# One lot of values per pair of heads, the maximum taken before a copy, and two output products interleaved

## The reference, cut to what matters

```python
def even_mixer(h_lat, h_ctx, ...):
    ...                                   # keys and values: context and latent tokens joined, 768 in all
    def merge(o_a, o_b):
        return jnp.dot(jnp.concatenate([o_a, o_b], axis=-1), w_out)
    out_lat = merge(attend(mla_q(...), ka, va), attend(gqa_q(...), kb, vb))
    out_ctx = merge(attend(mla_q(... ctx), ka_c, va_c), attend(gqa_q(... ctx), kb_c, vb_c))

def attend(q, k, v):                      # per block of 128 queries and per head
    s = einsum(q, k) * scale
    p = softmax(s)
    return einsum(p, v)

x = x + gt1 * out_lat
ctx = ctx + cgt1 * out_ctx
```

## Time and profile before

| | us |
|---|---|
| runs of the kernel before | 3757.66, 3762.18, 3762.24; median 3762.18 |
| profiled execution, device time | 3759.26 |
| its span, first to last instruction | 3757.9 |
| PE busy over the span | 3628.1 (97%) |
| DVE, ACT, POOL busy | 2474.8 (66%), 1597.5 (43%), 259.1 (7%) |
| mean granted TensorE clock | 0.974 of full speed |

### The profile page before, as it was taken

How to read it: one execution, slowest core, us unless ns; L and a number is a source line. 1 busy time by engine, 2 the same in 40 slices (tenths; PEclk the granted TensorE clock), 3 DMA queues, 4 the chain that set the end, 5 groups by cost and what they waited for, 6 DMA issues and landing times.

```text
span 3757.9 us, 53327 instructions
## 1 busy us (share of the span) xinstructions
PE 3628.1 (97%) x21516; PEld 3086.6 (82%) x21516; DVE 2474.8 (66%) x3727; ACT 1597.5 (43%) x2587; POOL 259.1 (7%) x197
## 2 busy tenths in 40 slices
PE   7999999999999998999999999999999999979999
PEld 4866778888888866788889987899978999659998
DVE  5445667755547255544598877888756887478886
ACT  3246643323135234323354446544444444475443
POOL 0000104830000010000000011000020000100000
PEclk8999999999999989999999999999999999999999
DMA  5210022433322101223233332333323334203332
GB/s 211 99 32 1 2 88 83 133 125 127 121 86 74 58 29 42 83 95 101 90 96 102 102 107 79 96 102 101 96 91 124 111 103 146 63 16 93 106 106 91
DMA packets 276309, 338.94 MB, mean 90 GB/s; under 512 B 15456, under 2 KB 197344, under 8 KB 275424
## 3 DMA queue, kind: packets, MB, share of 16 engines
q1 hardware_dynamic: 272752, 320.40, 27.4%
q10 hardware_dynamic: 3312, 15.13, 1.1%
HBM read 329.18 MB, written 6.29 MB: 89 GB/s over the span
## 4 chain that ended last, share of the span: by engine, by line
PE 82%; DVE 7%; ACT 2%; issue 2%; DMA 0%; SPq 0%; POOL 0%; ACTq 0%; DVEq 0%
PE ps L843 15%; PE ps L845 15%; PE ps L844 15%; PE ps L1667 7%; PE ps L1669 7%; PE ps L1668 7%; PE ps L2128 1%; PE ps L2102 1%; PE ps L1987 1%; PE ps L1988 1%; PE ps L1989 1%; DVE t L442 1%; PE ps L2092 1%; PE ps L3259 1%; PE ps L3257 1%
## 5 line engine op out<-in xcount | busy, mean ns | idle before, releaser
L843 PE MATMUL ps<-t 128*128 128x512 f32 (+1 forms) x2236 | 806.2, 361 | 10.4 <-DVE t L2853 6.5
L844 PE MATMUL ps<-t 128*128 128x512 f32 (+1 forms) x2236 | 801.5, 358 | 0.0
L845 PE MATMUL ps<-t 128*128 128x512 f32 (+1 forms) x2236 | 800.4, 358 | 0.0
L429 ACT ACTIVATE t<-t 128x1024 fp32r<-128x1024 f32 (+2 forms) x438 | 437.1, 999 | 588.6 <-PE ps L845 367.3
L442 DVE TENSOR_TENSOR t<-t 128x1024 fp32r<-128x1024 f32 (+2 forms) x438 | 506.2, 1157 | 244.7 <-ACT t L429 242.0
L1667 PE MATMUL ps<-blocks_hi,t 128*128 128x256 f32 x1888 | 533.0, 282 | 16.2 <-ACT t L1696 12.1
L1668 PE MATMUL ps<-blocks_lo,t 128*128 128x256 f32 x1888 | 528.8, 280 | 0.0
L1669 PE MATMUL ps<-blocks_hi,t 128*128 128x256 f32 x1888 | 528.7, 280 | 0.0
L843 PEld LDWEIGHTS ps<-t 128*128 128x128 f32 x2236 | 426.6, 191 | 75.6 <-issue 10.7
L845 PEld LDWEIGHTS ps<-t 128*128 128x128 f32 x2236 | 426.3, 191 | 62.2
L844 PEld LDWEIGHTS ps<-t 128*128 128x128 f32 x2236 | 426.8, 191 | 61.2 <-issue 1.1
(11 more groups left out here) (499 smaller groups left out, 6274.6 us busy)
## 6 DMA issues: line engine op xcount, KB each, us to landing
t<-w_s_up SPq DMA_DIRECT2D x184, 256.0 KB, 3.6
t<-w_up SPq DMA_DIRECT2D x88, 512.0 KB, 3.6
raw_more<-w_s_up SPq DMA_DIRECT2D x168, 256.0 KB, 3.5
t<-w_ada SPq DMA_DIRECT2D x160, 256.0 KB, 3.1
raw_more<-w_s_down SPq DMA_DIRECT2D x72, 256.0 KB, 2.7
t<-w_down SPq DMA_DIRECT2D x32, 512.0 KB, 3.6
t<-w_s_down SPq DMA_DIRECT2D x56, 256.0 KB, 2.7
t<-w_ada SPq DMA_DIRECT2D x16, 512.0 KB, 10.6
```

The costliest lines, as they stand in the source:

```text
L429: k.A.activation(self.pair(n)[0], self.slot(self.raw_at[n])[:, 0:self.size(n)], ACT.Copy)\
L843: k.T.matmul(out, wh, hh, start=(i == 0), stop=False)
L844: k.T.matmul(out, wh, hl, start=False, stop=False)
L845: ins = k.T.matmul(out, wl, hh, start=False, stop=(i == len(kts) - 1))
```

## The change

In `PairUnits`: `pe_spread` is merged into `pe_values`, and a pair's values are done in one lot in the even step, after the spread; the odd step has scores and transposes alone. DVE takes the maximum of unit i before it copies unit i-2, and forms the result of a pair in the even step, behind that copy. In `ProjectOut`, which gets a flag `paired` that only the first attention sets, the first two blocks are done side by side: `dense_two` goes over kt and does three matmuls for block 0 and three for block 1, first for the latent tokens, then for the context tokens; both weight blocks are let go of when all four products are done. The next blocks are as before.

```diff
 class ProjectOut:
+    def made(self, m, si):
+        if self.paired and m < 2:
+            return self.done.at(2 * si + m + 1)
+        return self.done.at(self.ns * m + si + 1)
+
+    def pe_pair(self):
+        k, st = self.k, self.k.stream
+        weights = [st.operand(self.c + m, self.name, m) for m in range(2)]
+        for si, mix in enumerate(self.mixes):
+            outs = []
+            for m in range(2):
+                i = self.ns * m + si
+                self.bank[i], before = k.banks.take(self.res.at(i + 1))
+                k.pe.wait_ge(before)
+                outs.append(self.bank[i][:, 0:(NL, NC)[si]])
+            dense_two(k, outs, weights, mix.k, lambda kt: self.ready(si, kt), (self.done, self.done))
+        for m in range(2):
+            st.used[self.c + m] = self.done.at(2 * self.ns)
+
     def pe(self, between=None):
         k, st = self.k, self.k.stream
+        if self.paired:
+            self.pe_pair()
         for m in range(8):
-            w = st.operand(self.c + m, self.name, m)
+            w = st.operand(self.c + m, self.name, m) if m > 1 or not self.paired else None
             if between:
                 between(m)
+            if w is None:
+                continue
...
-                k.dve.wait_ge(self.done.at(i + 1))
+                k.dve.wait_ge(self.made(m, si))
...
-            if 0 <= i - 4 < n:
-                if i % 2 == 0:
-                    self.pe_spread((i - 4) // 2)
-                self.pe_values((i - 4) // 2, i % 2)
+            if i % 2 == 0 and 0 <= i - 4 < n:
+                self.pe_values((i - 4) // 2)
...
-    def pe_values(self, p, part):
+    def pe_values(self, p):
...
-        for c in range(part * nb // 2, (part + 1) * nb // 2):
+        for c in range(nb):
...
-        if part:
-            ins.then_inc(self.pv.sem, 1)
+        ins.then_inc(self.pv.sem, 1)
...
         for i in range(n + 4):
+            if i < n:
+                self.dve_max(i)
             if 0 <= i - 2 < n:
                 self.dve_keep(i - 2)
-            if i < n:
-                self.dve_max(i)
-            if i % 2 and 0 <= i - 4 < n:
+            if i % 2 == 0 and 0 <= i - 4 < n:
                 self.dve_result((i - 4) // 2)
```

More of the change, by code:

```diff
@@ L1902, with __init__ @@
 class ProjectOut:
-    def __init__(self, k, name, mixes, ready, scale, scale_ready, following=None):
+    def __init__(self, k, name, mixes, ready, scale, scale_ready, following=None, paired=False):
         self.k, self.name, self.mixes, self.ready, self.scale, self.scale_ready = k, name, mixes, ready, scale, scale_ready
+        self.paired = paired
         self.done, self.res = k.event("out_done"), k.event("out_residual")
@@ L2104, in pe_turn @@
         ins.then_inc(self.tn.sem, 1)
-    def pe_spread(self, p):
-        k = self.k
-        k.pe.wait_ge(self.fin.at(p))
-        k.pe.wait_ge(self.rc.at(2 * p + 2))
-        for half in range(2):
-            ins = k.T.matmul(k.ps[64 * half:64 * half + 64, 6 + (p + 1) % 2, 128:256],
-                             self.recip(p)[:, half:half + 1].broadcast_to([P, 64]), k.ident, start=True, stop=True)
-        ins.then_inc(self.rb.sem, 1)
-    def pe_values(self, p, part):
+    def pe_values(self, p):
         k = self.k
@@ L2120, in pe_values @@
         b = k.ps[:, 6 + p % 2, :]
+        k.pe.wait_ge(self.fin.at(p))
+        k.pe.wait_ge(self.rc.at(2 * p + 2))
+        for half in range(2):
+            ins = k.T.matmul(k.ps[64 * half:64 * half + 64, 6 + (p + 1) % 2, 128:256], self.recip(p)[:, half:half + 1].broadcast_to([P, 64]),
+                             k.ident, start=True, stop=True)
+        ins.then_inc(self.rb.sem, 1)
         k.pe.wait_ge(self.rk.at(p))
@@ L2829, in even_mixer @@
             out = ProjectOut(k, "att_out", [M, MC], lambda si, kt: hl.at(8 * si + kt + 1), lambda m, si: k.mod(0, 2, m, si),
-                             ada.ready(0, 2), lambda finished: Gather(k, finished, 2))
+                             ada.ready(0, 2), lambda finished: Gather(k, finished, 2), True)
             def pe_program():
```

## The result

The changed kernel takes 3766.25 us (median of 14 runs, 3754.87 to 3770.93) beside 3758.26 us (14 runs, 3753.24 to 3762.24) for the kernel before. The profiled spans are 3764.7 and 3757.9 us, 6.8 apart as well.

A forecast was written before the change was run, and what follows sets the result against it. PE was taken to set the pace, DVE and ACT mattering only as latencies. Latent rounds -2.2, grouped rounds +4.8 and projection +2.1 summed to +4.7 us, forecast 3765.4 us, range 3750 to 3774.

The forecast's parts named there:

- The copy binds on grouped heads: Grouped even steps: transposes wait 0.46 us for DVE's copy behind the maximum; a pair takes 5.16 for 4.97.
- The ends of the wide run: First narrow and first wide units of a round: grouped transposes wait 0.92, 0.47 and 1.3 us for copies.
- the loop of 2.74: Grouped heads, DVE's path from scores through maximum and copy until PE can start the transposes: 2.74 us.
- Sum of the attention: Attention stage: grouped rounds lose 4.8 us, latent rounds gain 2.2, together +2.6 us.
- A change of output width costs 0.12 and 0.16: PE groups beside a 64/128-column change cost 0.12 and 0.16 us more; one lot saves 0.28 a pair.
- the margin of 0.11: Latent heads, start of scores to next transposes: PE's path 3.43 us, DVE's 3.32, so no wait, whole saving kept.
- Projection: PE waits 2.1 us at L807: Column sums ahead of block 3 wait for DVE's last multiply-add after the late weight release; cost +2.1 us.
- the upper bound of 3.7: Projection: the most its wait could cost, 3.7 us, if SyncE's second tile takes 5.1 us.
- Rival 1: Attention: the copy doesn't bind, every pair gets its 0.28 us; 3748.0 to 3750.9 us; chance 0.20.
- Rival 2: Attention: DVE's result waits in every wide pair for ACT's spread copy; +9.6, 3773.6 to 3776.5 us; chance 0.18.
- Rival 3: Projection: its wait isn't there; 3761.9 to 3764.8 us; within the forecast's case of 0.62.
- rival 4: Projection: side by side doesn't cover a wait on DVE's low halves; the forecast itself, within its 0.62.

The follow-up runs named there:

- e4: Kernel after without the side-by-side products, so both attention changes against the kernel before; 3763.87 us, ratio 1.0017.
- e5_lot_copy_first: Kernel before with values in one lot and the result in the even step, copy still ahead of maximum, no pair; 3757.95 us, ratio 1.0001.
- e3_pair_only: Kernel before with only the first two output products side by side, attention unchanged; 3757.36 us, ratio 1.0000.
- e6: Kernel after without the pair of products and with DVE's result back in the odd step; a single run, 3758.71 us.
- e9: Kernel before with lots, mixed DVE order and even-step result on latent heads, halves with maximum first on grouped heads, no pair; 3750.26 us, ratio 0.9978.

## Why the prediction was right, and where its terms were not

Forecast +4.7 us, same by the 0.2% that was set, measured +6.8 (4.1 to 9.4), inside the range. The 0.2%, 7.5 us, was too coarse a bound for what can be told from no change: the interval is 2.6 us to either side and leaves out zero. The mechanisms it named are there; the sizes of both stages were about half of what was measured.

1. *The copy binds on grouped heads.* Right. The loop was costed at 2.74 from scores to transposes and 5.16 a pair; it is 2.83 and 5.29. Until the maximum begins 1.02 (as forecast), maximum to negation 0.99 for 0.97, then copy and PE's going on 0.69 for 0.62: the estimate of 0.06 for PE to go on was 0.14. Another 0.04 are in transposes and lot.
2. *The ends of the wide run.* Right in place, small in size: waits of 1.19, 0.96 and 0.50 where 1.3, 0.92 and 0.47 were forecast. By thirds a grouped round is 7.47 + 11.24 + 8.30 for 7.6 + 11.1 + 8.0, a latent one 8.93 + 11.73 + 8.69 for 9.1 + 11.7 + 8.4. The narrow third fails by 0.3 in both. The nearness of the waits is in part chance, since they are counted in two ways. The forecast's 0.92 is, but for rounding, what the loop of 2.74 leaves beside 1.81 of PE from start to start; counted so, the wait is 1.12 (442.31 less 440.86 less 0.33), because the loop is 2.82 (439.49 to 442.31) and scores with transposes take 1.37 instead of 1.48. The idle time in a row, 0.96, counts from the modelled end of the scores. On latent heads the rows show 0.76 and 0.31 for 0.73 and 0.28, with the same reserve.
3. *Sum of the attention.* +5.5 for +2.6. The grouped rounds give 0.97 + 1.73 + 1.73 + 2.05 = +6.5 for +4.8, the latent ones +0.38 - 0.44 - 0.43 - 0.52 = -1.0 for -2.2. The +0.38 is the first round, which starts while the clock comes up: it takes 32.71 and 32.41 us in the two profiles of before, at a granted clock of 0.84 and 0.95. After has 0.38 more at the first of these clocks and e4, with the same attention, 0.91 less at the second, so it tells nothing. Without it the attention loses 5.1. The latent rounds gain 0.43 to 0.52 and not 0.7, since their narrow third is 0.3 longer than reckoned (item 2).
4. *A change of output width costs 0.12 and 0.16.* Mis-sized: 0.35 a pair without waits (e5_lot_copy_first). The kernel after doesn't get it even on latent heads: the transposes of its even steps start 1.37 after the scores, not 1.29: DVE's loop, from scores to transposes, is 3.42 (349.26 to 352.68) for 3.32, while PE alone needs 3.34 (347.82 to 351.16 in e5), not 3.43. So the margin of 0.11 that I gave latent heads wasn't there, and the pair takes 5.87, not 5.77.
5. *Projection: PE waits 2.1 us at L807.* Right to the row (2.10), with its cause, the last multiply-add. The cost of the stage is 4.6, for two things that were not in the sum. Block 3 takes 10.05 for 8.44 at the lower clock: +1.6. And L807 is reached 27.55 us after the first product (543.00 less 2.10, less 513.35), 26.70 before (534.13 less 507.43): +0.8. The projection begins at the lower level in every kernel, behind a gap of 6.5 us on PE; here it stayed there longer, with a granted clock of 0.50 and 0.89 in its first two stretches of 4 us for 0.56 and 1.00 in e3_pair_only, which reaches L807 after 26.9. That part isn't the pair's: e6 and e9, with the projection of before, take 27.6. The pair's own cost is 2.1 + 1.6 = 3.7, just at the upper bound of 3.7, which had been reckoned for another reason (a late tile).
6. *Whole kernel.* 10.1 in the stages against 6.8 in the time. At equal clock the kernel after is 8.1 slower, give or take 0.9. Of the 10.1, 2.4 are low clock (1.6 in block 3, 0.8 at the projection's start), and the 7.7 left are within that error. The forecast was nearer to the result than its terms were to theirs (2.6 for 5.5, 2.1 for 4.6), and that is luck.

Rival 1 (the copy doesn't bind) falls by the rows at 437.03 and 431.75. Rival 2 (the result in every wide pair) doesn't come about: in a steady pair DVE's result waits for the values (1.08 us, at 439.68, released by L2148) and not for the spread copy, and the next maximum begins 1.02 after its scores, as forecast. With the copy first it does come about: in e5_lot_copy_first the result waits 1.31 us for the spread copy in a steady grouped pair. Rival 3 falls by the row of L807, rival 4 is shown: with the wait gone, side by side is worth nothing.

What stays open: how much of the 4.0 us of the projection reaches the end. They aren't made up for soon: by DVE's instructions, the profile of e3_pair_only loses 4.0 us on that of before from 507 to 579 us and still has 3.8 of them at 1110. Its time doesn't show them (1.0000, at most 3.4 slower). At equal clock, which takes out the 1.6 of low clock, 2.1 should be left: e3 has +0.9, give or take 1.5, and the kernel after beside e4_attention_only, which differ in the pair alone, +2.8, give or take 1.4. Both fit 2.1, neither measures it. The runs of e3 drew a slightly higher clock (0.9755), and nothing here tells whether by chance. Nor is it settled why the first 8 us of the projection differ in their clock from kernel to kernel.

## What to carry to other kernels

Merging two halves into a lot saves what stands between them on the busy engine, but it also removes the cover that the second half gave to others: list, for each bank and buffer that the lot touches, who must have read it (here the copy and the result) and where that reader now stands in its engine's program. An order of two instructions that is right in one step can be wrong in the next, so try it by parity and by kind of work: here lots in mixed order on latent heads, halves with the maximum first on grouped ones and no pair of products gave a ratio of 0.9978, where the change as made had 1.0018. And set times of a few us in thousands against the mean granted clock of each run before believing them either way.

## What the runs showed of the hardware

- The spread between runs of one kernel goes mostly with the granted clock: 2.1 us for each 0.001 of its mean, correlation -0.85 over 212 runs, and two profiles of one kernel differ by 0.06 in the same 90 us.
- Two changes a pair between 64 and 128 columns of output, with the matmuls the same, cost 0.35 us: a steady latent pair takes 6.12 us with them and 5.77 without, and PE waits in neither.
- A pause of 2.10 us on PE, with 1.9 us of one-column matmuls behind it, was followed by some 3.5 us at the lower clock level (0.57 in the window of 545 to 549, matmuls of 0.63 for 0.39 us), in both kernels that had it (0.65 from 539.5 to 544 in e3_pair_only). In the eleven profiles without the pause the clock stayed at 1.00 behind the column sums. In the grouped round of the kernel after, with pauses of up to 1.19 us, it was 1.00 too. So a wait of 2.1 us cost 3.7.
